# Five norms whose first projections take the unscaled input, with the squares added up on GpSimd

## The reference

```
def rmsnorm(x, g):
    xf = x.astype(jnp.float32)
    y = xf * lax.rsqrt(jnp.mean(xf * xf, axis=-1, keepdims=True) + RMS_EPS)
    return (y * g.astype(jnp.float32)).astype(x.dtype)
```

## Time and profile before

| | us |
|---|---|
| median of 3 runs | 1772.78 |
| lowest, highest | 1770.03, 1773.89 |
| the profiled execution | 1774.91 |
| its span, first to last instruction | 1773.0 |
| TensorE busy in it | 1590.0 |
| VectorE busy | 741.3 |
| ScalarE busy | 398.9 |
| GpSimd busy | 285.8 |

### The profile page before, as it was taken

The page is one execution under the profiler, slowest core; times in us unless marked ns, Lnnn a source line. Parts: engine busy times, 40 slices in busy tenths (PEclk is TensorE's granted clock), DMA queues, the critical chain, the costliest instruction groups (busy, mean ns, idle before and its releaser), DMA issues. The chain is left out here.

```text
span 1773.0 us, 18216 instructions
## 1 busy us (share of the span) xinstructions
PE 1590.0 (90%) x6378; PEld 1141.5 (64%) x6378; DVE 741.3 (42%) x1946; ACT 398.9 (23%) x944; POOL 285.8 (16%) x285
## 2 busy tenths in 40 slices
PE   7999999999777777777779899999989999999997
PEld 6888866454223322223257788888878877788886
DVE  2102566676667776675534432121131134312213
ACT  1110122222222222222134221111113134211111
POOL 0000033334443434344203001000000000000000
PEclk9999999999999999999999999999999989999999
DMA  6443299999999999999923135434424310443440
GB/s 254 145 164 120 91 402 418 426 426 421 427 426 427 427 427 427 426 416 418 395 81 114 47 133 221 147 142 160 159 75 139 107 39 1 168 152 142 151 167 25
DMA packets 56164, 419.14 MB, mean 236 GB/s; under 512 B 6372, under 2 KB 6692, under 8 KB 10048
## 3 DMA queue, kind: packets, MB, share of 16 engines
q0 software_dynamic: 38240, 274.83, 37.2%
q1 hardware_dynamic: 17856, 143.46, 22.0%
HBM read 416.19 MB, written 1.09 MB: 235 GB/s over the span
## 5 line engine op out<-in xcount | busy, mean ns | idle before, releaser
L1453 PE MATMUL wide<-arena 128*128 128x512 f32 x1024 | 473.7, 609 | 120.6 <-ACT arena L459 120.4
L1292 PE MATMUL bank<-hT,wring 128*128 128x256 f32 (+2 forms) x2512 | 559.8, 383 | 15.7 <-DVE hT L825 15.7
L1292 PEld LDWEIGHTS bank<-hT,wring 128*128 128x128 f32 (+2 forms) x2512 | 472.6, 189 | 94.2 <-issue 17.4
L1453 PEld LDWEIGHTS wide<-arena 128*128 128x128 f32 x1024 | 188.8, 192 | 393.7 <-ACT arena L459 198.3
L967 DVE CUSTOM_DVE_ANT_0 arena<-arena,wide 128x1024 f32<-128x1024 f32 x256 | 312.5, 1221 | 192.8 <-DMA arena<-uv_dram,arena 192.5
L413 POOL DMA_INDIRECT arena<-uv_dram,arena x256 | 257.6, 1006 | 481.0 <-PE wide L1453 284.5
L1137 DVE SCALAR_TENSOR_TENSOR arena<-bank,prm,arena 128x254 f32<-128x254 f32 (+1 forms) x176 | 76.7, 477 | 340.8 <-ACT arena L459 334.9
L459 ACT ACTIVATE arena<-arena 128x2 f32<-128x2 f32 (+3 forms) x196 | 66.9, 344 | 525.3 <-DVE arena L967 439.6
L1630 PE MATMUL wide<-arena,wring 128*128 128x256 f32 x704 | 159.3, 379 | 1.2 <-DVE arena L1151 1.2
L1630 PEld LDWEIGHTS wide<-arena,wring 128*128 128x128 f32 x704 | 133.6, 190 | 20.0 <-DVE arena L1151 2.0
L459 ACT ACTIVATE arena<-bank,prm 128x256 f32<-128x256 f32 (+1 forms) x96 | 48.2, 552 | 320.0 <-PE bank L1292 318.9
(11 more groups left out here) (190 smaller groups left out, 1138.1 us busy)
## 6 DMA issues: line engine op xcount, KB each, us to landing
wring<-ffn_dram SPq DMA_DIRECT2D x44, 1536.0 KB, 6.5
wring<-win_dram SPq DMA_DIRECT2D x16, 1024.0 KB, 4.8
wring<-wout_dram SPq DMA_DIRECT2D x8, 1024.0 KB, 4.7
wring<-wout_dram SPq DMA_DIRECT2D x4, 1280.0 KB, 5.7
wring<-mix_dram SPq DMA_DIRECT2D x4, 1024.0 KB, 4.7
wring<-wqd_dram SPq DMA_DIRECT2D x4, 1024.0 KB, 10.7
arena<-uv_dram,arena POOLq DMA_INDIRECT x256, 12.2
wring<-memkv_dram SPq DMA_DIRECT2D x4, 1024.0 KB, 9.4
```

The costliest lines, as they stand in the source:

```text
L1292: ins = MM(b[0:rows, m * S:(m + 1) * S], w[:, (m * kt + k) * width:(m * kt + k) * width + rows], src[:, k, :], start=k == 0, stop=k == kt - 1)
L1453: ins = MM(wide[:, 2 + h, :], diag[:, n % 4, e, :], G[:, r % NBUF, D + 512 * h:D + 512 * (h + 1)], start=r % (HEADS * TOPK) == 0, stop=r % ...
```

## The change

At mean_x, mean_ffn, mean_f0, mean_kv and mean_f1, VectorE first multiplies x by the gain (`gain`, a tensor_scalar into xg0, xgF or xgE, two per piece of x, right behind the addition that completes the piece). The leading groups (wina 0 and 1; wqa; ffn groups 0 and 1; kvc 0 and 1) take this product (`raw`: k outermost, both output tiles inside). VectorE writes the reciprocal of the root to an SBUF tile, rstd (`inverse`), and multiplies the finished PSUM group by it (`scale`), after which the group's taker reads it as before (wqa is now taken by VectorE itself). The normed hT (at mean_kv xn1 too) is still written, for all later groups (`finish`).

The mean is put inside the first of these groups, behind its sixth k step. GpSimd adds the squares up (`fold`: three additions of 128x512, in place, chained), so the mean has two matmuls (`mean_folded`). The memory's mean is folded too, and its norm moves from behind mean_ffn to behind the first four groups of win; on VectorE it now stands ahead of the pooling. mean_fin, mean_mix0 and mean_out keep their old form, except that behind a feed-forward VectorE now waits after each of its four additions for that addition.

The order on VectorE is inverse, scale of the first group, finish, scale of the second group, and only then the next stage's work; at mean_kv the finish of xn1 comes between the two scales and that of hT behind. The token rows move behind wqb. At the start g_mix moves from prm to cst, and prm is issued behind the second slot of win.

```
+            def gain(dst, src, col, k):
+                V.tensor_scalar(dst[:, k, :], src[:, k, :], col[:, k:k + 1], None, ALU.mult).then_inc(gained, 1)
+            def inverse(stage):
+                b = full(stage)
+                norm.n += 1
+                dve.wait_ge(rooted, norm.n)
+                V.reciprocal(rstd[:], b[:, 0:S]).then_inc(freed[DVE_], 1)
+                dve.wait_ge(freed[DVE_], TAKEN[GROUP0[stage]])
+            def scale(stage, i=0):
+                b = full(stage, i)
+                V.tensor_tensor(halves(b), halves(b), rstd[:].unsqueeze(1).broadcast_to([128, 2, S]), ALU.mult).then_inc(scaled, 1)
+            def finish(dst, src, col):
+                for k in range(KT):
+                    V.scalar_tensor_tensor(out=dst[:, k, :], in0=src[:, k, :], scalar=col[:, k:k + 1], in1=rstd[:],
+                                           op0=ALU.mult, op1=ALU.mult).then_inc(normed, 1)
...
+            def fold(sq_, before):
+                for n in range(1, 4):
+                    pool.wait_ge(squared, before + n + 1)
+                    if n > 1:
+                        pool.wait_ge(folded, fold.n)
+                    nc.gpsimd.tensor_tensor(sq_[:, 0:2, :], sq_[:, 0:2, :], sq_[:, 2 * n:2 * n + 2, :], ALU.add).then_inc(folded, 1)
+                    fold.n += 1
...
+            def raw(w, src, b, before, mean=None):
+                for k in range(KT):
+                    pe.wait_ge(gained, before + k + 1)
+                    for m in range(2):
+                        ins = MM(b[:, m * S:(m + 1) * S], w[:, (m * KT + k) * 128:(m * KT + k + 1) * 128], src[:, k, :],
+                                 start=k == 0 and m == 0, stop=k == KT - 1 and m == 1)
+                    if k == 5 and mean:
+                        mean_folded(*mean)
+                return ins
+            def mean_folded(stage, src, folds):
+                b = begin(stage)
+                pe.wait_ge(folded, folds)
+                for k in range(2):
+                    ins = MM(b[:, 0:S], C("mean_d", 128), src[:, k, :], start=k == 0, stop=k == 1)
                 ins.then_inc(group_full, 1)
...
-            def add_groups(stage):
+            def add_groups(stage, dst, col):
...
                     dve.drain().then_inc(freed[DVE_], 1)
+                    dve.wait_ge(added, add_groups.n)
+                    for k in range(2 * i, 2 * i + 2):
+                        gain(dst, xT, col, k)
...
-            add_groups("wout0")
-            norm("mean_f0", xT, [(hT, "norm_ffn", 0)])
+            add_groups("wout0", xgF, P("norm_ffn", 0, 8))
+            inverse("mean_f0")
+            scale("ffn0", 0)
+            finish(hT, xT, P("norm_ffn", 0, 8))
+            scale("ffn0", 1)
...
-                up(0, 0, norms)
+                up(0, 0, mean)
+                up(1, 1)
+                down(0, 0)
+                pe.wait_ge(normed, norms)
                 with pe.Fori(0, (FT - 2) // 4) as i:
                     up.i = i
                     for s in range(4):
-                        up(i * 4 + (s + 1), s + 1)
-                        down(i * 4 + s, s)
-                up(FT - 1, FT - 1)
-                down(FT - 2, FT - 2)
+                        up(i * 4 + (s + 2), s + 2)
+                        down(i * 4 + (s + 1), s + 1)
```

More of the change, by code:

```diff
@@ L60 @@
     for _s in range(_c):
-        if _name in ("win", "wqa", "wqb", "wqc", "wqd", "wout", "wout0", "wout1", "memkv", "kvc", "nsamq", "nsagl"):
+        if _name == "win":
+            USED.append(("group", GROUP0["wina"] + _s + 1 if _s < 4 else GROUP0["win"] + _s - 3))
+        elif _name in ("wqa", "wqb", "wqc", "wqd", "wout", "wout0", "wout1", "memkv", "kvc", "nsamq", "nsagl"):
             USED.append(("group", GROUP0[_name] + _s + 1))
@@ L1163, in ffn @@
                                     xT[:, 2 * n:2 * n + 2, :], ALU.add).then_inc(added, 1)
-                add_groups.n += 4
-                dve.wait_ge(added, add_groups.n)
-            ffn("ffn0", 0)
-            norm("mean_kv", xT, [(hT, "kv_norm", 0), (xn1, "norm_mix", 8)])
+                    add_groups.n += 1
+                    dve.wait_ge(added, add_groups.n)
+                    if layer == 0:
+                        for k in range(2 * n, 2 * n + 2):
+                            gain(xgE, xT, P("kv_norm", 0, 8), k)
+            ffn("ffn0", 0)
+            inverse("mean_kv")
+            scale("kvc", 0)
+            finish(xn1, xT, P("norm_mix", 8, 8))
+            scale("kvc", 1)
+            finish(hT, xT, P("kv_norm", 0, 8))
             steps(V.memset(kcblk, 0.0))
@@ L1252, in _ @@
                     nsa_max(J + 3)
-            add_groups("wout1")
-            norm("mean_f1", xT, [(hT, "norm_ffn", 8)])
+            add_groups("wout1", xgF, P("norm_ffn", 8, 8))
+            inverse("mean_f1")
+            scale("ffn1", 0)
+            finish(hT, xT, P("norm_ffn", 8, 8))
+            scale("ffn1", 1)
             ffn("ffn1", 1)
@@ L1340, in _ @@
                 done(project(slot("wout", i), mT, b))
-            mean("mean_ffn", sq, 8)
-            mean("mean_mem", sqm, 4)
-            pe.wait_ge(normed, 16)
             def token_rows(t):
@@ L1609, in _, with ffn @@
                 done(ins)
-            def ffn(stage, layer, norms):
+            def ffn(stage, layer, norms, gains, mean):
                 g0, n0, k0 = GROUP0[stage], SLOT0[stage], layer * FT
@@ L1645, in ffn @@
                 ins.then_inc(f_sum, 1)
-            mean("mean_f0", sqF, 20)
-            ffn("ffn0", 0, 48)
-            mean("mean_kv", sqE, 24)
+            ffn("ffn0", 0, 56, 16, ("mean_f0", sqF, 12))
             for i in range(2):
-                b = begin("kvc", i)
-                done(project(slot("kvc", i), hT, b, norms=None if i else 56))
+                w = slot("kvc", i)
+                done(raw(w, xgE, begin("kvc", i), 24, None if i else ("mean_kv", sqE, 15)))
             b = begin("nsamq")
-            done(project(slot("nsamq", 0), xn1, b, norms=64))
+            done(project(slot("nsamq", 0), xn1, b, norms=56))
             b = begin("nsagl")
@@ L1816, in _ @@
                 wout1(KT - 1, half)
-            mean("mean_f1", sqF, 28)
-            ffn("ffn1", 1, 72)
+            ffn("ffn1", 1, 80, 32, ("mean_f1", sqF, 18))
             mean("mean_out", sqF, 32)
```

112 lines of the change are left out of this document (75 added, 37 removed).

## The result

The changed kernel takes 1762.93 us, median of 4 runs (1761.16 to 1763.46); the kernel before, run beside it, 1773.34 (1770.03 to 1774.39). The ratio is 0.9942, 95% interval [0.9929, 0.9954]. The forecast was 1753.3: the sign was right, the size nearly twice too large (19.5 us foreseen, 10.4 measured). The profiled execution took 1763.46 us, its span 1761.7.

What follows compares the result with a forecast made beforehand. TensorE (busy 90%) was taken to bound the kernel, saturated DMA the gathers from 235 us. Terms 2.9 + 8.2 - 0.1 + 7.0 + 1.5 = 19.5 us, against the median 1772.8, gave 1753.3; range 1747 to 1763.

Steps and rivals of the forecast that it cites:

- start: First projection: no mean ahead of it, TensorE starting at about 10.7 us; 2.9 us earlier (bounds 2.3 to 3.6).
- mean_ffn and gathers: Second norm: VectorE starts selecting 8.2 us earlier, so the first gather and the DMA-saturated stage behind it move by 8.2 us.
- mean_f0: First feed-forward's norm: 1.5 us gained up to the first `down`, 1.6 charged for the clock behind a new wait: -0.1 us.
- mean_kv: Norm ahead of kvc: raw products run while additions are still made; nsamq ends at 1338.6 instead of 1345.6, 7.0 us earlier.
- mean_f1: Second feed-forward's norm: 22.2 us becomes 19.05 (15.7 plus a wait of 3.35), less 1.6 for the clock: 1.5 us gained.
- a longer gather stage: Sign that the prediction is wrong: the gather stage's length grows, where it was to move whole by 8.2 us.
- 1.0 us for an addition: GpSimd's 128x512 additions of squares: 1.0 us each (bounds 0.69 and 3.8), ending a TensorE wait only at mean_kv, by 0.5.
- The waits before the first `down`: Both feed-forwards: TensorE waits 3.35 us after up 1 for VectorE's scaling and tile 0, then loses 1.6 to the clock.
- The 15.6 us of mean matmuls: Six means with 2 calls instead of 8, 0.432 us a call: 15.6 us of TensorE work, an upper part of the sum.

Runs made afterwards that it cites:

- e3: Changed kernel with the first weight slot of ffn1 loaded early, beside kvs, into free space of its own: 1754.59 us, ratio to the kernel before 0.9888.
- e8: Changed kernel with mean_f1 in its old form and the first ffn1 weight slot loaded early: 1755.73 us, ratio to the kernel before 0.9896.
- e2: Changed kernel with mean_f1 alone put back to its old form: 1756.95 us, ratio to the kernel before 0.9904.
- The repeats: The changed kernel run twice more without any edit: 1760.14 us on chip B and 1758.54 us on chip A, ratios to the kernel before 0.9929 and 0.9916.
- e4: Changed kernel with e1's and e3's edits together: 1744.16 us and, run again, 1745.21; ratios to the kernel before 0.9835 and 0.9832.
- e1: Changed kernel with VectorE doing tile 0 before finishing hT and scaling group 1, in both feed-forwards: 1747.76 us, ratio to the kernel before 0.9854.
- e5: Changed kernel without GpSimd's adding up of squares, each mean again eight matmuls inside the raw group: 1775.54 us, ratio to the kernel before 1.0017.
- e6: Kernel before with only the squares of the six norms folded on GpSimd, norms and order unchanged: 1786.35 us, ratio to the kernel before 1.0079.
- e9: e6 with 20 matmuls on zeros put ahead of each folded mean: 1776.92 us, ratio to the kernel before 1.0019.
- e7: Changed kernel with mean_f0 alone put back to its old form: 1761.10 us, ratio to the kernel before 0.9933.

## Why the prediction was wrong, step by step

Shifts between the profile before and the one of the result, in us (positive: earlier):

| step | forecast | measured | |
|---|---|---|---|
| start | 2.9 | 3.0 | T at 189.77 and 186.76 |
| mean_ffn and gathers | 8.2 | 4.3 | less the start's 3.0: 8.5 at the first gather, 6.9 at the last (869.05, 859.19), 4.3 where mean_fin is through |
| mean_f0 | -0.1 | 0.0 | |
| mean_kv | 7.0 | 6.9 | |
| mean_f1 | 1.5 | -2.8 | |
| sum | 19.5 | 11.3 | spans 1773.0 and 1761.7; the rows, rounded, add up to 11.4 |

**The step that failed is mean_f1's.** The prediction put it: "After: the same 15.7 + 3.35 = 19.05: 3.1 us." It took mean_f0's working over although one thing differs: at ffn1 the first weight slot is free only when wout1's first group is through. The transfer of 6.3 us lay under mean, root, reciprocal and multiplications (9.0 us) and was seen nowhere. The change took that cover away, and the transfer came out as a wait of 2.9 us, with a group 1.5 us slower behind it: 4.4 us, the 4.3 between forecast and measurement. e3 and e8 show that it is the transfer, and e2 what the place costs. The row was in the trace before the change: SyncE's queue at ffn1's weights from 1518.74 on, with the shortest landing 6.4 later. For the start I had asked when the weights land, here I had not.

**mean_ffn and the gathers.** The mechanism held: the first gather came 11.5 us earlier (2.9 + 8.2 = 11.1 forecast), and DMA carried it. Behind it 4.2 us were lost: 1.3 from the first to the ninth gather, with the late copy in between, 0.4 to the last one, 0.9 from there to the last sum, and 1.7 in mean_fin, where 16 instructions of the mean took 5.38 us instead of 3.69 with PEclk at 0.72 from 882 to 888. None of these places was changed. On chip A mean_fin is through at 889.18 against 900.40, 11.2 earlier (2.4 of it from the start), and there the time stands 15.4 us below the kernel before, as 19.5 less mean_f1's 4.3 would have it. This compares with a profile of before whose chip isn't named. The repeats agree that the losses vary with the program unchanged: mean_fin's 16 instructions took 3.69 us in both, and 5.38 again in e4 on chip A. On chip B, with the late copy, mean_fin stands 9.7 us earlier than before, 3.2 of that from the start. So I put these losses down to chip and execution, not to the change. That is argued from one profile of the kernel before; the late copy's cause is open, so about half of the missing 8.2 us is shown (mean_f1) and half is not. The prediction's own sign of error, a longer gather stage, came in the result's execution (first to last gather 649.3 us, 647.6 before) and not on chip A (646.5).

**GpSimd.** I took 1.0 us for an addition; it is 1.26 to 1.40, inside the bounds. It ended one wait of TensorE, 0.54 us at mean_kv, as forecast, and two of VectorE's pairs of gains beside it took 1.14 and 0.92 us instead of 0.62, 0.5 and 0.3 more where 0.3 was foreseen. The largest such delays stand at the start, where the prediction had none: three of the eight gains took 1.22 to 1.35 us instead of 0.34. They cost nothing, because TensorE's first groups wait for weights until 10.71.

**The waits before the first `down`** came at both ffn stages with 3.0 us (forecast 3.35) and 1.8 of clock behind (1.6); the granted clock was 0.59 over 1530 to 1534, not the 0.50 expected. e1 removes both, worth 9.6 us by the rows: the forecast saw this wait and priced it right, and of what the experiments took away it was the largest.

**What bounds the gain.** The 15.6 us of mean matmuls, the sum's upper part, are what the fold saves inside the new order (15.4, e5). But the fold by itself costs 14 us (e6), and the new order by itself 3.2. Together they give 12.2 on that chip. My reading is that the raw groups fill TensorE's wait for GpSimd; e9, which fills it with zeros and gets 11 of the 14 us back, supports it.

## What to carry to other kernels

When a wait is taken away, look at what ran under it: list every transfer whose buffer comes free just before, and compare its landing with the new date at which it is asked for. Work taken off TensorE pays only if something else fills the time: here it came back from 3.97 us of idling at half its clock, and two edits that each lose gained together. And when products move ahead of a scaling, order the other engine by who waits: the first tile before the rest of the norm took off another 10.8 us, beside the 15.4 of the change on the same chip.

## What the runs showed of the hardware

- An in-place addition of 128x512 f32 on GpSimd took 1.26 us alone and up to 1.40 beside VectorE's multiplications in the profiled execution of the result.
- A multiplication of 128x256 on VectorE that began while such an addition ran took 1.22 us (6.78 to 8.00, the addition 6.58 to 7.84) and 0.88 us (1311.01 to 1311.89, the addition 1310.47 to 1311.74) instead of 0.34: each ended some 0.15 us behind the addition.
- The same wait of 2.99 us before mean_f1's first `down` was followed by 5.41 us for 16 instructions in the three executions of the changed kernel and 3.72 in e3; a wait of 3.04 us for weights by 5.42 for 24 (e1) or 8.42 (e7), one of 2.89 by 6.82; waits of 2.1 to 2.2 us too were followed by 15.67 for 64 instructions (e2), or by 14.05 (e9).
- On one chip a copy of ScalarE beside the gathers came 1.5 us late in both executions that were kept, and the ninth gather at 239.6 us; on the other it was on time in all seven, with the ninth gather at 236.1 to 236.7.
